# Score products of a sliding-window attention: query parts stacked, key parts doubled, four 128-row matmuls in place of six 64-row ones

## The reference: what is computed

```python
q = qkv[..., :D].reshape(B, nb, BLOCK, N_KV_HEADS, G, HEAD_DIM) * (HEAD_DIM ** -0.5)   # nb = 4 blocks of 128
kb, vb = band(k), band(v)                                      # 3 key blocks for each query block
s = jnp.einsum('bnqhgd,bnjhd->bhgnqj', q, kb)                  # HEAD_DIM = 64
s = jnp.where(mask, s + bias, finfo.min)                       # |i - j| <= 128, T5 bias
m = jnp.maximum(jnp.max(s, -1), sink)
p = jnp.exp(s - m); p = p / (sum(p) + exp(sink - m))
o = jnp.einsum('bhgnqj,bnjhd->bnqhgd', p, vb)
```

## Time and profile before

| | |
|---|---|
| median of 3 runs | 1150.6 us (1150.18 to 1153.1) |
| the profiled execution | 1150.15 us |
| its span | 1148.5 us |
| TensorE (PE) busy | 1136.8 us, 99% |
| VectorE (DVE) busy | 629.9 us, 55% |
| ScalarE (ACT) busy | 504.9 us, 44% |
| GpSimd (POOL) busy | 137.7 us, 12% |
| mean DMA rate | 93 GB/s |
| granted TensorE clock | 0.998 of full speed |

### The profile page before, as it was taken

One profiled execution on the slowest core, in us unless ns is written; L12 is line 12 of the kernel. 1 busy time (PEld: TensorE's weight loads), 2 busy tenths in 40 slices (PEclk: granted clock), 3 DMA queues, 4 the chain that ended last, 5 costly groups with the idle time before them and its releaser, 6 DMA issues.

```text
span 1148.5 us, 16697 instructions
## 1 busy us (share of the span) xinstructions
PE 1136.8 (99%) x5648; PEld 938.1 (82%) x5648; DVE 629.9 (55%) x1020; ACT 504.9 (44%) x908; POOL 137.7 (12%) x239
## 2 busy tenths in 40 slices
PE   8999999999999999999999999999999999999997
PEld 6888888888888888888887878888888888888886
DVE  7778887764442234444345778766444223444333
ACT  6777777553431124333324666645343112333221
POOL 6544341240000000000000322100000000000000
PEclk9999999999999999999999999999999999999999
DMA  6332321333222322332222112122322332232222
GB/s 219 100 91 83 99 87 58 92 119 103 98 92 94 108 92 91 99 102 83 99 91 92 47 55 61 52 74 93 108 92 92 96 105 92 91 104 97 91 92 92
DMA packets 34291, 106.98 MB, mean 93 GB/s; under 512 B 5760, under 2 KB 8096, under 8 KB 34256
## 3 DMA queue, kind: packets, MB, share of 16 engines
q1 hardware_dynamic: 29344, 98.61, 26.0%
q0 software_dynamic: 4768, 7.90, 2.9%
q10 hardware_dynamic: 144, 0.02, 0.0%
HBM read 103.84 MB, written 2.67 MB: 93 GB/s over the span
## 4 chain that ended last, share of the span: by engine, by line
PE 98%; DVE 1%; DMA 0%; ACT 0%; issue 0%; DVEq 0%; ACTq 0%
PE acc L395 29%; PE acc L396 28%; PE acc L397 28%; PE s_ps L498 3%; PE om_ps L532 2%; PE pt_ps L702 2%; PE om_ps L556 1%; PE om_ps L528 1%; PE pt_ps L519 1%; PE om_ps L488 1%; PE s_ps L395 1%; PE s_ps L396 1%; PE s_ps L397 1%; DVE w_lo L1074 0%; DMA w_raw<-in_wstream 0%; PE om_ps L541 0%
## 5 line engine op out<-in xcount | busy, mean ns | idle before, releaser
L796 ACT CAST w_hi<-w_raw 128x1024 fp32r<-128x1024 f32 x180 | 189.1, 1051 | 405.1 <-PE acc L397 398.0
L395 PE MATMUL acc<-h_hi,w_hi 128*128 128x512 f32 x792 | 318.3, 402 | 0.7 <-DVE w_lo L1074 0.7
L397 PE MATMUL acc<-h_hi,w_lo 128*128 128x512 f32 x792 | 309.0, 390 | 0.0
L396 PE MATMUL acc<-h_lo,w_hi 128*128 128x512 f32 x792 | 308.9, 390 | 0.0
L1074 DVE TENSOR_TENSOR w_lo<-w_raw,w_hi 128x1024 fp32r<-128x1024 f32 x178 | 218.8, 1229 | 143.3 <-ACT w_hi L796 142.7
L395 PE MATMUL acc<-u_hi,w_hi 128*128 128x512 f32 (+1 forms) x624 | 241.3, 387 | 0.0
L397 PE MATMUL acc<-u_hi,w_lo 128*128 128x512 f32 (+1 forms) x624 | 239.5, 384 | 0.0
L396 PE MATMUL acc<-u_lo,w_hi 128*128 128x512 f32 (+1 forms) x624 | 239.5, 384 | 0.0
L395 PEld LDWEIGHTS acc<-h_hi,w_hi 128*128 128x128 f32 x792 | 148.7, 188 | 37.1 <-issue 4.2
L397 PEld LDWEIGHTS acc<-h_hi,w_lo 128*128 128x128 f32 x792 | 148.7, 188 | 31.7
L396 PEld LDWEIGHTS acc<-h_lo,w_hi 128*128 128x128 f32 x792 | 148.9, 188 | 28.3 <-issue 0.7
(11 more groups left out here) (135 smaller groups left out, 1019.3 us busy)
## 6 DMA issues: line engine op xcount, KB each, us to landing
w_raw<-in_wstream SPq DMA_DIRECT2D x180, 512.0 KB, 3.3
bias_pairs<-rpb_reversed POOLq DMA_DIRECT2D x64, 62.0 KB, 2.4
bias_pairs<-t_shifted POOLq DMA_DIRECT2D x64, 48.0 KB, 2.1
x_res<-in_xT SPq DMA_DIRECT2D x8, 256.0 KB, 5.7
out_y<-x_res SPq DMA_DIRECT2D x8, 128.0 KB, 1.8
out_y<-x_res SPq DMA_DIRECT2D x4, 256.0 KB, 2.3
t_shifted<-vT POOLq DMA_DIRECT2D x16, 31.0 KB, 2.1
mask<-in_mask POOLq DMA_DIRECT2D x1, 64.0 KB, 5.2
```

What stands on the lines that cost most here:

```text
L395: nc.tensor.matmul(dst, a[0], b[0], start=start, stop=False)
L396: nc.tensor.matmul(dst, a[0], b[1], start=False, stop=False)
L397: return nc.tensor.matmul(dst, a[1], b[0], start=False, stop=stop)
L796: nc.scalar.copy(w_hi[:, c.odd, :], w_raw[:, c.odd, :]).then_inc(w_hi_made, 1)
```

## The change

Each head gets its own stack of 128 rows: for queries the high part of the head in one half and its low part in the other (`q_stack`), for keys the high part in both halves (`k_stack_hi`) and the low part in both halves (`k_stack_lo`). A score product is then two matmuls of 128 rows for each head: stack times doubled high keys, and stack times doubled low keys, which adds the product low*low as well. The query stacks use slots 8 and 9 of `u_hi` and `u_lo` as before, the high keys `k_hi` and `k_lo`, the low keys slots 10 to 13 of `u_hi`. ScalarE and VectorE make the parts half by half, and for half of them the output lies on the other 64 partitions than the input.

```diff
+        HEAD_ROWS = (TOP, BOTTOM)
+        def q_stack(odd, hh):
+            return (u_lo if hh else u_hi)[:, 8 + odd, :]
+        def k_stack_hi(kv, hh):
+            return (k_lo if hh else k_hi)[:, kv, :]
+        def k_stack_lo(kv, hh):
+            return u_hi[:, 10 + 2 * kv + hh, :]
...
                 kb, nb = SW_BLOCKS[n]
-                head_products(lambda hh: s_ps[:, hh, 0:nb * P], (8 + p.odd, slice(P * n, P * (n + 1))),
-                              (p.odd, slice(P * kb, P * (kb + nb)))).then_inc(scores_done, 1)
+                for hh in range(2):
+                    queries, keys = q_stack(p.odd, hh)[:, P * n:P * (n + 1)], slice(P * kb, P * (kb + nb))
+                    nc.tensor.matmul(s_ps[:, hh, 0:nb * P], queries, k_stack_hi(p.odd, hh)[:, keys], start=True, stop=False)
+                    ins = nc.tensor.matmul(s_ps[:, hh, 0:nb * P], queries, k_stack_lo(p.odd, hh)[:, keys], start=False,
+                                           stop=True)
+                ins.then_inc(scores_done, 1)
...
+            def queries_high(m):
+                act.wait_ge(acc_taken, (m + (GR_SW + 5)).v)
+                src = scaled[:, m.odd, :]
+                nc.scalar.copy(q_stack(m.odd, 0)[TOP, :], src[TOP, :])
+                nc.scalar.copy(q_stack(m.odd, 1)[BOTTOM, :], src[BOTTOM, :]).then_inc(tile_hi, 1)
+            def keys_high(kv):
+                act.wait_ge(acc_taken, GR_SW + 2 * kv + 1)
+                src = scaled[:, kv, :]
+                for hh in range(2):
+                    for half in HEAD_ROWS:
+                        ins = nc.scalar.copy(k_stack_hi(kv, hh)[half, :], src[HEAD_ROWS[hh], :])
+                ins.then_inc(tile_hi, 1)
...
             def queries_low(m):
-                tile_low(m + (TI_SW + 2), u_lo[:, 8 + m.odd, :], u_hi[:, 8 + m.odd, :])
+                dve.wait_ge(tile_hi, (m + (TI_SW + 3)).v)
+                for hh in range(2):
+                    own, other = HEAD_ROWS[hh], HEAD_ROWS[1 - hh]
+                    ins = nc.vector.tensor_tensor(q_stack(m.odd, hh)[other, :], scaled[own, m.odd, :],
+                                                  f32(q_stack(m.odd, hh)[own, :]), ALU.subtract)
+                ins.then_inc(tile_split, 1)
+            def keys_low(kv):
+                dve.wait_ge(tile_hi, TI_SW + kv + 1)
+                for hh in range(2):
+                    for half in HEAD_ROWS:
+                        ins = nc.vector.tensor_tensor(k_stack_lo(kv, hh)[half, :], scaled[HEAD_ROWS[hh], kv, :],
+                                                      f32(k_stack_hi(kv, hh)[HEAD_ROWS[hh], :]), ALU.subtract)
+                ins.then_inc(tile_split, 1)
```

More of the change, by code:

```diff
@@ L1023, in sw_step @@
                     if n == 2 and dense:
-                        tile_high(m + (GR_SW + 4), m + (TI_SW + 2), u_hi[:, 8 + m.odd, :])
+                        queries_high(m)
                     if n == 3:
@@ L1047, in _ @@
             split_weights(At(CH_SW + 2))
-            tile_high(At(GR_SW), At(TI_SW), k_hi[:, 0, :])
+            keys_high(0)
             split_weights(At(CH_SW + 3))
             split_weights(At(CH_SW + 4))
-            tile_high(At(GR_SW + 2), At(TI_SW + 1), k_hi[:, 1, :])
+            keys_high(1)
             v_high(At(UNITS_NA), v_hi[:, 0:4, :, :])
@@ L1054, in _ @@
             split_weights(At(CH_SW + 6))
-            tile_high(At(GR_SW + 4), At(TI_SW + 2), u_hi[:, 8, :])
+            queries_high(At(0))
             v_high(At(UNITS_NA + 1), v_hi[:, 4:8, :, :])
@@ L1436, in _ @@
             split_weights(At(CH_SW + 2))
-            tile_low(At(TI_SW), k_lo[:, 0, :], k_hi[:, 0, :])
+            keys_low(0)
             dve.wait_ge(t5_stored, 16 * QC)
@@ L1442, in _ @@
             split_weights(At(CH_SW + 4))
-            tile_low(At(TI_SW + 1), k_lo[:, 1, :], k_hi[:, 1, :])
+            keys_low(1)
             v_low(At(UNITS_NA), slice(0, 4))
```

## The result

The changed kernel takes 1152.75 us (median of 13 runs, 1152.35 to 1154.14), the kernel before, beside it, 1150.51 us (13 runs). The ratio is 1.0021, with a 95% interval of 1.0014 to 1.0027. The profiled execution took 1152.37 us with a span of 1150.7, which is 2.2 us above the span of before; the forecast was 2.35.

The account below looks back on a forecast made before the run. TensorE was taken to bound now (98% of the span), VectorE's loop after. Way in 1.41 - 0.2, six periods 0.84 and keys 0.3 give +2.35 us: 1152.5 us, range 1149.4 to 1156.5.

Parts of the forecast that it names:

- The loop: Second attention, VectorE's steps from one pair's subtraction to the next pair's: 16.05 us, 0.14 more than now; 60 in 100.
- subtraction to the query's low part: Second attention, from a unit's subtraction to the start of the query's low part: 1.68 and 0.09, 1.77 us.
- output sums: VectorE after the query subtractions: 1.48 us; the earlier 0.33 wait for TensorE goes because VectorE comes later.
- transposes to subtraction: Within the pair's loop, from a unit's transposes to the next subtraction: 1.28 us.
- on to the next pair's first unit: Within the loop, all VectorE: a split of weights, logits and sums, 4.28 us.
- TensorE's saving: Second attention's score products: four of 128 rows replace six of 64, 0.86 us less a pair, TensorE needing 15.05.
- the fourth rival: Score units: the 0.36 us beyond streaming stays, 0.60 more a pair, total 1156.7 us; 10 in 100.
- Half operations: Queries' casts and subtractions alternating partition halves lose their overlap: 0.70 us each on VectorE, 0.64 on ScalarE.
- The second rival: Query splitting: half operations overlap as full ones do, loop 15.78 us, way in 1.1, total 1150.5; 14 in 100.
- the third rival: The gain comes through: TensorE's 15.05 us sets the pair, for example through shorter 64-row subtractions; total 1145 us; 6 in 100.
- The way in: First pair, nothing hides the queries' splitting: first scores 1.41 us later, +1.2 us at the second pair's start.
- Keys: Key splitting, one cast and one subtraction become four each; TensorE waits about 0.3 us for the split weights.

Follow-up runs that it names:

- The third subtraction: Changed kernel with a third 64x512 subtraction, its output unused, behind the two of each query tile: 1159.04 us, ratio 1.0074, the pair 16.783.
- the split's move: First unit's weight split put ahead of the subtractions on VectorE: changed kernel 1151.18 us, pair 15.867; kernel before 1150.47 us, pair 15.933.
- the kernel with the splitting alone: Kernel before, old products kept, queries' cast and subtraction done in two halves of 64 partitions: 1153.72 us, ratio 1.0032.
- the one with the products alone: Changed kernel with new products, queries and keys cast and subtracted in one piece as before, each head's own scores left out: 1147.4 us, ratio 0.9976.
- The kernel with both on one half: Changed kernel with both query casts and both subtractions on the upper 64 partitions, low parts to unused space: 1149.86 us, ratio 0.9995.
- the fastest kernel: Changed kernel with weight split moved ahead, a signal after the first query cast, and the outputs' denominators moved out of the output sums: 1146.53 us, ratio 0.9964.

## Why the prediction was right

The forecast was +2.35 us and +2.2 came, by the mechanism forecast. The loop, step by step from the timeline above, beside the sum of the prediction:

| step | forecast | measured |
|---|---|---|
| subtraction to the query's low part (698.84 to 700.63) | 1.77 | 1.79 |
| two subtractions (to 702.04) | 1.40 | 1.41 |
| output sums (to 703.52) | 1.48 | 1.48 |
| subtraction, values, transposes (to 705.92) | 2.42 | 2.40 |
| transposes to subtraction (to 707.20) | 1.28 | 1.28 |
| on to the next pair's first unit (691.15 to 695.44) | 4.28 | 4.29 |
| and to its third (to 698.84) | 3.42 | 3.40 |
| a period | 16.05 | 16.05 |

The mean over six pairs is 16.08. The third subtraction (+0.706 a pair) and the split's move (faster after, nothing before) show that this loop is what binds, and that it doesn't bind in the kernel before. One reading behind it was wrong: the prediction says that VectorE waits only 0.2 to 0.3 us at a time, and its own have a wait of 0.79 at 705.02. The sum was spared, since it takes that step whole, from the transposes to the subtraction, with the wait in it.

**TensorE's saving** was forecast as 0.86 a pair and is 0.96: the term was a little small, because a unit of 256 columns takes 0.93 - 0.48 = 0.45 and one of 384 takes 0.70. It didn't matter, since the loop took it. The 0.36 us beyond the streaming are gone, so the fourth rival, by which they stay, falls. They belong to the half-array form: the kernel with the splitting alone keeps the old products and them, the one with the products alone is rid of them. Where they lie is seen in the starts of the kernel before, between the rows:

```profile
692.69 0.44 PE L498 MATMUL s_ps<-k_hi,u_hi 64*128 64x384 f32 x2
...
693.41 0.50 PE L395 MATMUL acc<-h_hi,w_hi 128*128 128x512 f32 x1
```

The first scores start 0.32 behind the dense product at 692.37 (0.08 more than its 0.24), the six take 0.72 (0.18 more than three slots of 0.18), and the second dense product starts 0.34 behind the first (0.10 more): 0.36, in parts on the way in and out. The weight loads stand idle at both changes, and the changed kernel has neither line in its waits:

```profile
PEld s_ps L498 <- issue: 11.0, 30, 0.4
PEld acc L395 <- issue: 4.0, 16, 0.3
```

That is 0.37 us of idle loads ahead of 30 units and 0.25 behind 16 of them; it marks the two changes and is not itself the time lost. The Trainium skill's TensorEngine Tiling (Array Packing), Key Properties, says that a change of the tiling mode drains TensorE; the trace agrees, with the 0.36 us between the starts. The Trainium skill's rule in TensorE: Matmul & The Clock Gate, Part 3, that products of few rows belong into separate row groups, doesn't pay here: three slots and the change of form cost 0.90 and 0.73, four full products 0.70 and 0.45.

**Half operations.** The second rival, that they overlap as full ones do, falls: 0.70 from start to start, as taken. The kernel with both on one half and the one with the splitting alone show the cause. The Trainium skill's section Two Vector instructions with no wait between them (VectorE: DVE Perf Modes) describes a held instruction, and the trace agrees in detail: the small addition, which reads SBUF from partition 0 behind a subtraction that read from 64, starts 0.71 after it (702.04 - 701.33); the reduction in the fastest kernel, which reads only PSUM, starts 0.61 after the same subtraction (698.60 - 697.99).

**The gain comes through**, the third rival, fell for the changed kernel. It is true in part for the fastest one, by another way than the prediction named: not a shorter subtraction, but two tiny operations out of the loop. Its 15.05 a pair was reached by none: 15.33 is the least, 0.36 above TensorE's 14.97. With the old splitting it is 15.57. The waits left in the fastest kernel (4.1 us for line 1157) say that VectorE's subtraction still holds the values up; which path does it there was not taken apart.

**The way in.** The first scores were forecast 1.41 later and are 625.92 - 624.53 = 1.39 later. The timeline of all engines in the changed kernel answers to the earlier trace rows:

```profile
622.49 0.61 ACT L873 CAST u_hi<-scaled 64x512 fp32r<-64x512 f32 x1
...
623.11 0.62 ACT L874 CAST u_lo<-scaled 64x512 fp32r<-64x512 f32 x1
...
623.75 0.69 DVE L1415 TENSOR_TENSOR u_hi<-scaled,u_hi 64x512 fp32r<-64x512 f32 x1 [1.47 <-ACT u_lo L874]
...
625.17 0.69 DVE L1152 TENSOR_TENSOR v_parts<-om_ps,v_parts 128x512 fp32r<-128x512 f32 x1
...
625.92 0.39 PE L708 MATMUL s_ps<-k_hi,u_hi 128*128 128x256 f32 x1 [1.23 <-DVE v_parts L1152]
```

Of the 1.39, 0.11 came in with the first cast (622.49, before 622.38) and comes from the keys, as the next paragraph shows. So this term measured 1.28 us, 0.13 less than forecast: the first low part starts 623.75 - 622.49 = 1.26 behind the first cast, where 1.28 was taken, and the scores 625.92 - 625.17 = 0.75 behind V's low part, where 0.84 was. The second 384-column unit of the second pair starts at 646.13 against 644.84, 1.29 later, or 1.18 without those 0.11; 1.2 was forecast for this pair. The same unit of the last pair starts at 742.60 against 740.44, 2.16 later: the six periods brought 0.87, forecast 0.84.

**Keys.** This term was mis-sized: forecast 0.3 us, measured 0.15. The timeline of all engines in the changed kernel answers to the earlier trace rows:

```profile
603.07 1.25 ACT L882 CAST k_hi<-scaled 64x512 fp32r<-64x512 f32 x2 [3.08 <-DVE scaled L1137]
...
604.33 1.25 ACT L882 CAST k_lo<-scaled 64x512 fp32r<-64x512 f32 x2
...
605.62 1.38 DVE L1423 TENSOR_TENSOR u_hi<-scaled,k_hi 64x512 fp32r<-64x512 f32 x2 [1.45 <-ACT k_lo L882]
...
609.04 1.22 DVE L1108 TENSOR_TENSOR w_lo<-w_raw,w_hi 128x1024 fp32r<-128x1024 f32 x1
...
610.31 0.50 PE L409 MATMUL acc<-h_hi,w_hi 128*128 128x512 f32 x1
```

The first key cast stands at 603.07, 0.06 earlier than in the earlier trace rows: this execution was ahead by that much before anything of the change ran. TensorE's product that stood at 610.22 stands at 610.31, so the keys cost 0.09 + 0.06 = 0.15, and 0.17 where the queries begin. Counted from the first cast, the last one ends after 2.51 where 2.56 was forecast, and the split of weights starts after 5.97, as forecast. What was too much is mostly the release: TensorE starts 0.05 behind the end of the split (609.04 + 1.22 = 610.26), where 0.15 was taken. The 0.13 too many of this term and the 0.06 that this execution was ahead are the 0.19 between the sum, 2.35, and the 2.16 of the last pair.

## What to carry to other kernels

Before an engine is given less work, add up the loop that starts and ends at one instruction and runs through every engine whose order is fixed, with the new operations in it; an engine that is 55% busy can be 0.4 us a period from taking over (15.93 before, and 15.57 as soon as TensorE has its new products and nothing else is changed). If it would, look in that loop for small operations whose inputs are long there: moving two of them was worth more than twice the loss of this change, and nothing without it. Operations on half the partitions take as long as on all of them, and alternating the halves costs their overlap as well.

## What was not expected of the hardware

An addition of four elements with two inputs in SBUF took 1.27 us beside a GpSimd subtraction that also reads SBUF, instead of 0.16, and a scaling 0.90 instead of 0.42; operations with one input in PSUM were not slowed. The Trainium skill has this in SBUF — State Buffer, section Who interferes with whom: such a VectorE instruction and a GpSimd one that reads SBUF shut each other out for a whole instruction. The trace agrees: the addition ended at 702.67 and GpSimd's subtraction at 702.65. GpSimd was busy 12% in the kernel before, and that says nothing of this price, nor of the 1.28 us that its subtraction of 64x512 takes where VectorE's takes 0.69.

The gains are not additive: splitting alone +3.3 us, products alone -3.0, both together +2.2. The pair shows it too: 16.205 with the splitting alone, 15.565 with the products alone, 16.077 with both. In these sums the keys' own 0.15 is in the last alone.
